# First transfers of a fused transformer-layer kernel cut and reordered, with three matmuls on a cleared region ahead

## What is computed

```python
def rms_norm(x, g):
    y = x * lax.rsqrt(jnp.mean(x * x, axis=-1, keepdims=True) + EPS)
    return y * g

h = rms_norm(x, mix_norm)
z = h @ w_in                      # columns: attn q,k,v | ret q,k,v,gate | gates A,B
aq, ak, av, rq, rk, rv, rg, ga, gr = split(z)
rq, rk = apply_rope(rq), apply_rope(rk)
merged = sigmoid(ga) * attention(aq, ak, av) @ w_o_att + sigmoid(gr) * norm_gate(retention(rq, rk, rv), rg) @ w_o_ret
x = x + merged @ w_out
x = x + peer(rms_norm(x, ffn_norm))                       # top-k experts, gathered
x = x + sigmoid(rms_norm(x, ple_norm) @ w_ple_gate) * (p @ w_ple_proj)
return rms_norm(x, final_norm)
```

## Time and profile before

| | us |
|---|---|
| Median of 3 runs | 1992.97 |
| Lowest and highest | 1991.73 and 1994.1 |
| Profiled execution, whole | 1998.92 |
| Its span (first to last instruction) | 1997.1 |
| TensorE busy in the span | 1961.2 |

### The profile page before, as it was taken

The page is one execution under the profiler, slowest core; times in us unless marked ns, Lnnn a source line. Parts: engine busy times, 40 slices in busy tenths (PEclk is TensorE's granted clock), DMA queues, the critical chain, the costliest instruction groups (busy, mean ns, idle before and its releaser), DMA issues.

```text
span 1997.1 us, 28913 instructions
## 1 busy us (share of the span) xinstructions
PE 1961.2 (98%) x10211; PEld 1725.5 (86%) x10211; DVE 1313.9 (66%) x2287; ACT 803.8 (40%) x1273; POOL 1226.6 (61%) x682
## 2 busy tenths in 40 slices
PE   7999999999999999999999999999999999999997
PEld 6888888888888888999999999999888888888886
DVE  6433333333732389988967888861897898888846
ACT  6222222233553333443345666663343333333352
POOL 5342424243234333898877666667899888888821
PEclk9999999999999999999999999999999999999998
DMA  6232313242223332999987999999999999999921
GB/s 210 74 112 62 115 59 107 72 137 80 80 85 95 103 118 79 332 339 329 353 307 258 392 362 365 372 384 315 350 380 387 370 363 355 366 362 363 357 64 43
DMA packets 171953, 471.93 MB, mean 236 GB/s; under 512 B 13776, under 2 KB 62928, under 8 KB 170064
## 3 DMA queue, kind: packets, MB, share of 16 engines
q1 hardware_dynamic: 58032, 209.04, 30.9%
q0 software_dynamic: 41472, 151.01, 19.9%
q10 hardware_dynamic: 72352, 110.64, 15.8%
HBM read 413.49 MB, written 54.53 MB: 234 GB/s over the span
## 4 chain that ended last, share of the span: by engine, by line
PE 69%; DMA 10%; DVE 9%; POOL 8%; issue 2%; ACT 1%; DVEq 0%; SPq 0%; ACTq 0%; POOLq 0%
PE bank L923 22%; PE bank L925 21%; PE bank L924 21%; DMA xT<-peer_down,scr 9%; POOL w_lo L488 6%; POOL xT L512 3%; DVE xT L1303 3%; PE bank L1031 1%; PE bank L1114 1%; DMA gate_scratch<-scr 1%; PE bank L1099 1%; DVE b_hi L1659 1%; DMA raw<-weights 1%; PE bank L1075 0%; PE bank L1085 0%
## 5 line engine op out<-in xcount | busy, mean ns | idle before, releaser
L488 POOL TENSOR_TENSOR w_lo<-raw,w_hi 128x1024 fp32r<-128x1024 f32 x390 | 936.9, 2411 | 570.1 <-ACT w_hi L538 566.0
L923 PE MATMUL bank<-h_hi,w_hi 128*128 128x352 f32 (+2 forms) x1560 | 550.9, 353 | 9.7 <-ACT scr L743 8.9
L925 PE MATMUL bank<-h_hi,w_lo 128*128 128x352 f32 (+2 forms) x1560 | 539.2, 346 | 0.0
L924 PE MATMUL bank<-h_lo,w_hi 128*128 128x352 f32 (+2 forms) x1560 | 538.2, 345 | 0.0
L538 ACT ACTIVATE w_hi<-raw 128x1024 fp32r<-128x1024 f32 x390 | 405.9, 1053 | 283.1 <-DMA raw<-weights 139.4
L923 PEld LDWEIGHTS bank<-h_hi,w_hi 128*128 128x128 f32 x1560 | 294.4, 189 | 31.9 <-POOL w_lo L488 7.3
L924 PEld LDWEIGHTS bank<-h_lo,w_hi 128*128 128x128 f32 x1560 | 295.3, 189 | 19.8
L925 PEld LDWEIGHTS bank<-h_hi,w_lo 128*128 128x128 f32 x1560 | 293.7, 188 | 20.9
L923 PE MATMUL bank<-w_hi,b_hi 128*128 128x512 f32 x768 | 298.8, 389 | 0.0
L925 PE MATMUL bank<-w_hi,b_lo 128*128 128x512 f32 x768 | 298.8, 389 | 0.0
L924 PE MATMUL bank<-w_lo,b_hi 128*128 128x512 f32 x768 | 298.8, 389 | 0.0
(11 more groups left out here) (215 smaller groups left out, 2446.9 us busy)
## 6 DMA issues: line engine op xcount, KB each, us to landing
raw<-weights SPq DMA_DIRECT2D x390, 512.0 KB, 5.4
act_scratch<-scr ACTq DMA_DIRECT2D x64, 384.0 KB, 5.8
gate_scratch<-scr ACTq DMA_DIRECT2D x12, 2048.0 KB, 12.7
scr<-gate_scratch ACTq DMA_DIRECT2D x22, 768.0 KB, 9.9
scr<-act_scratch ACTq DMA_DIRECT2D x22, 768.0 KB, 15.4
xT<-gate_scratch ACTq DMA_DIRECT2D x10, 768.0 KB, 9.1
xT<-act_scratch ACTq DMA_DIRECT2D x10, 768.0 KB, 13.8
scr<-scr ACTq DMA_DIRECT2D x20, 128.0 KB, 2.9
```

What stands on the lines that cost most here:

```text
L488: return nc.gpsimd.tensor_tensor(w_lo[:, s, :], raw[:, s % RAW, :], w_hi[:, s, :].bitcast(F32), ALU.subtract)
L923: nc.tensor.matmul(out, a_hi, c_hi, start=first, stop=False)
L924: nc.tensor.matmul(out, a_hi, c_lo, start=False, stop=False)
L925: return nc.tensor.matmul(out, a_lo, c_hi, start=False, stop=last)
```

## The change

The first transfers are cut and ordered anew. The norms' factors (columns 384 to 415 of `small`, 16 KB) go first under a semaphore of their own; weight unit 0 follows; x comes in five pieces of 1, 1, 2, 2 and 2 tiles, and weight unit 1 is issued between the third and the fourth; the rest of `small` comes in two pieces behind x, and weight units 2 and 3 last. ACT, DVE and TensorE wait for the parts they need. ACT makes `w_hi` of unit 1 after its sixth tile of x, no longer after the eighth. DVE first writes 1.0 into 640 columns of the scratch region, and TensorE runs three float32 matmuls of 512 columns on them, into a bank that is overwritten later.

```diff
--- before.py
+++ after.py
@@ -127,6 +127,10 @@
 S_AT = [sum(S - P * i for i in range(j)) for j in range(TT)]
 SMALL = 3 * P + 4 * KT + AH + 2 * NKEY
 SCRATCH = 15104
+GAINS = slice(3 * P, 3 * P + 4 * KT)
+X_PARTS = ((0, 1), (1, 2), (2, 4), (4, 6), (6, 8))
+X_PART = [i for i, (a, b) in enumerate(X_PARTS) for _ in range(a, b)]
+WARM = 3
 
 HALVES = (slice(0, S // 2), slice(S // 2, S))
 TD = S - P
@@ -349,8 +353,8 @@
         proj_free, pg_free = [sem("proj_free0"), sem("proj_free1")], sem("pg_free")
         tile_ready, tile_free = sem("tile_ready"), sem("tile_free")
 
-        x_landed = [sem(f"x_landed{i}") for i in range(KT // 2)]
-        small_landed = sem("small_landed")
+        x_landed = [sem(f"x_landed{i}") for i in range(len(X_PARTS))]
+        small_landed, gains_landed, warm_ready = sem("small_landed"), sem("gains_landed"), sem("warm_ready")
         rope_r_landed, rope_a_landed, p_landed = sem("rope_r_landed"), sem("rope_a_landed"), sem("p_landed")
         mask_landed = sem("mask_landed")
         decay_landed = [sem("decay_landed0"), sem("decay_landed1")]
@@ -463,11 +467,15 @@
 
         @block.sync
         def _(sp):
+            sp.dma_start(small[:, GAINS], small_d[:, GAINS]).then_inc(gains_landed, 16)
             sp.dma_start(raw[:, 0, :], w_d[0]).then_inc(landed[0], 16)
-            sp.dma_start(small[:, :], small_d).then_inc(small_landed, 16)
-            for i in range(KT // 2):
-                sp.dma_start(xT[:, 2 * i:2 * i + 2, :], xT_d[:, 2 * i:2 * i + 2, :]).then_inc(x_landed[i], 16)
-            for s in range(1, RAW):
+            for i, (a, b) in enumerate(X_PARTS):
+                sp.dma_start(xT[:, a:b, :], xT_d[:, a:b, :]).then_inc(x_landed[i], 16)
+                if b == 4:
+                    sp.dma_start(raw[:, 1, :], w_d[1]).then_inc(landed[1], 16)
+            for part in (slice(0, GAINS.start), slice(GAINS.stop, SMALL)):
+                sp.dma_start(small[:, part], small_d[:, part]).then_inc(small_landed, 16)
+            for s in range(2, RAW):
                 sp.dma_start(raw[:, s, :], w_d[s]).then_inc(landed[s], 16)
             with sp.Fori(1, NU // RAW) as r:
                 for s in range(RAW):
@@ -592,11 +600,12 @@
                 nc.scalar.activation(h_hi[:, k, :], normed[:, k % 2, :], ACT.Copy).then_inc(h_hi_ready, 1)
 
             run_ahead(0)
-            sc.wait_ge(small_landed, 16)
+            sc.wait_ge(gains_landed, 16)
             for k in range(KT):
-                sc.wait_ge(x_landed[k // 2], 16)
+                sc.wait_ge(x_landed[X_PART[k]], 16)
                 gained_upper(0, k, b_hi)
-            run_ahead(1)
+                if k == 5:
+                    run_ahead(1)
             for k in range(KT):
                 square(0, k)
                 if k == KT // 2:
@@ -604,6 +613,7 @@
             sc.dma_start(rope_r[:, :, :], rope_r_d).then_inc(rope_r_landed, 16)
             for i in range(2):
                 sc.dma_start(decay[:, i, :], decay_d[i]).then_inc(decay_landed[i], 16)
+            sc.wait_ge(small_landed, 32)
             root(0)
             run_ahead(RING - 1)
             for k in range(KT):
@@ -1008,11 +1018,14 @@
                     columns(("wor", i, m), b_hi, b_lo, kt=4, u=UNIT[("wor", 4 * i + m // 2)],
                             at=P * (m % 2), width=2 * P)
 
-            pe.wait_ge(small_landed, 16)
+            pe.wait_ge(warm_ready, 1)
+            for _ in range(WARM):
+                nc.tensor.matmul(bank[:, 7, :], cut(0, P), cut(P, S), start=True, stop=True)
             for i in range(RH):
                 values, gates_r = [("rv", i, t) for t in range(TT)], [("rg", i, t) for t in range(TT)]
                 if i == 0:
                     columns(("rq", 0), b_hi, b_lo, tiles=(u_ready, 0))
+                    pe.wait_ge(small_landed, 32)
                     columns(("rq", 1), b_hi, b_lo, at_tile={KT // 2: lambda: add_up(0), KT - 2: lambda: spread(0)})
                     for key in (("rk", 0), ("rk", 1)):
                         columns(key, b_hi, b_lo)
@@ -1415,10 +1428,12 @@
                 mark(tt(yacc[:, m, :], yacc[:, m, :], z, ALU.mult), tile_free)
 
 
-            ve.wait_ge(small_landed, 16)
+            nc.vector.memset(cut(0, P + S), 1.0).then_inc(warm_ready, 1)
+            ve.wait_ge(gains_landed, 16)
             for k in range(KT):
-                ve.wait_ge(x_landed[k // 2], 16)
+                ve.wait_ge(x_landed[X_PART[k]], 16)
                 gained_lower(0, k, b_lo, b_hi)
+            ve.wait_ge(small_landed, 32)
             for k in range(KT):
                 add_square(0, k)
             norm_scale(0)
```

## The result

| | before | after |
|---|---|---|
| Median of 19 runs each, us | 1991.99 | 1996.70 |
| Lowest and highest | 1987.88 and 1995.4 | 1993.88 and 2006.38 |
| Ratio, 95% interval | | 1.0022 [1.0013, 1.0031] |
| DVE's copy that ends the norm's chain | 24.03 | 27.99 |
| First scores of the retention | 60.08 | 64.00 |

The changed kernel is slower by 0.22% [0.13, 0.31], 4.4 us by the ratio and 4.7 by the medians. The forecast was 1994.8 (+1.85 us) in a range of 1991.0 to 1996.7: the time lies at the range's upper end, and the interval has the bound of 0.2% that was called no change inside it. Measured once more at the end, 7 runs against 17 other runs of the kernel before, it was 1.0026 [1.0014, 1.0038].

What follows compares the result with a forecast made beforehand. The prediction took x landing, ACT's tiles, the norm's chain and DVE's 18 us to bound the beginning, then TensorE to the end. Loads +0.65 and clock +1.2 gave +1.85 on 1992.97, so 1994.8, range 1991.0 to 1996.7.

Steps and rivals of the forecast that it cites:

- The path: At the start: x landing, ACT's tiles, squares, add_up, 1/rms, spread and DVE's 18 us set TensorE's steady work.
- TensorE's earlier start leads nowhere: Early matmuls: an earlier start and full clock gain nothing, as TensorE must follow the tiles; first real matmul 8.2 to 8.8.
- Term 1, the loads: Transfers and ACT's chain: the squares begin later, by +0.4 to +0.9 us, taken as +0.65.
- the landing of the first small pieces: First x transfers: landings follow the bytes ahead at 1.27 us per 512 KB, tiles 2 and 3 at 7.75 to 8.2.
- the overhead that the prediction weighed and left out: Factors' 16 KB transfer: small-transfer overhead, some 2 us, would make the sum 1.6 higher; taken as overlapping.
- Costs nothing by itself: ACT's w_hi of unit 1 between tiles 5 and 6: no cost, ACT's work ahead of the squares being the same sum.
- the waits for `small`: DVE's first sum (14.9) and TensorE's second rq pass (15.5): the waits cost nothing, small landing at 12.8.
- Term 2, the clock: TensorE behind a 2.9 us wait for the sum: half clock slows six matmuls and spread, 0 to +1.7, taken as +1.2.
- The sign given for it: In the profile after: if spread follows add_up by 2.4 us as before, the clock term is wrong.
- The forecast's copy: DVE's copy ending the norm's chain comes at 25.2 to 26.5, where it was at 24.03.
- The rival that forecast 1997.3: TensorE from 18 us on: two slow clock stretches make it last at the normalised tiles; +4.3 us, chance 0.07.
- the head start: ACT's first x tile: begins at 6.0 for 7.32; if it survives, -1.3 us, 1991.7, chance 0.14.

Runs made afterwards that it cites:

- e11: e5 with DVE making the normalised tiles ahead of the second rotation and the first values tile's lower part ahead of the keys' rotation; ratio 0.9992 [0.9978, 1.0006].
- e3: Changed kernel with ACT's w_hi of unit 1 back behind the eighth tile and unit 1's transfer issued behind all of x; ratio 1.0006 [0.9994, 1.0019].
- e5: Changed kernel with unit 1's transfer behind x, its w_hi behind the eighth tile, and the square root's table loaded early; ratio 1.0004 [0.9991, 1.0018].
- e2: Changed kernel with ACT's w_hi of unit 1 back behind the eighth tile, transfer order unaltered; ratio 1.0015 [0.9998, 1.0032].
- e1: Changed kernel with ACT's wait for the rest of small ahead of its three table transfers, not the square root; ratio 1.0020 [1.0008, 1.0031].
- e4: Changed kernel without DVE's fill and the three float32 matmuls; ratio 1.0019 [1.0007, 1.0031].
- e13: Changed kernel once more, unaltered, against other runs of the kernel before; ratio 1.0026 [1.0014, 1.0038].
- e6: Kernel before with DVE making the normalised tiles ahead of the second rotation, and ACT making w_hi of units 6 and 7 between its tiles; ratio 0.9991 [0.9976, 1.0005].
- e10: e6 on the kernel before, with DVE also making the first values tile's lower part ahead of the keys' rotation; ratio 1.0007 [0.9993, 1.0021].
- e12: e10 timed once more, against other runs of the kernel before; ratio 0.9995 [0.9985, 1.0005].
- e8: Kernel before with one more wait of ACT for small ahead of the square root; ratio 1.0005 [0.9993, 1.0018].

## Why the prediction came out as it did

**The path** was right: landing, ACT, squares, sum, 1/rms, `spread`, DVE's 18 us. The shift of the copy (3.96) is the shift at the scores (3.92), and experiments that moved the copy moved the scores by as much. That TensorE's earlier start leads nowhere held too, down to the waits for tiles; its first real matmul is at 8.96, a little past the 8.2 to 8.8 given, as POOL's lower part of unit 0 slows DVE's first two as well (2.55 us for the pair from 6.93).

**Term 1, the loads,** had the right cause and sign and was too small: +1.79 for +0.65 (0.4 to 0.9), or +1.3 by the means of all profiles. The step that failed is the landing of the first small pieces at 1.27 us for each 512 KB. Tiles 2 and 3 landed at 9.2 (7.75 to 8.2 forecast), tiles 4 and 5 at 11.7 (10.3 to 10.7). Between these two, 1024 KB took 2.5 us, so from there on the rate held, and the wait for the latter was right (1.15 for about 1.2); what was lost was lost by 9.2. The 16 KB ahead of everything landed 1.8 us from their issue but moved `w_hi` of unit 0 by 0.07 us only (4.79 for 4.72): the overhead that the prediction weighed and left out overlapped, as it took it to. (The last sum of bytes should read 3412 KB for 3420, which changes nothing.) The transfers of after move less in the first microseconds than those of before; the last number is GB/s, after first, then before:

```profile
4.00:6.00 2.00, 2.00 (x4) 0.67 (x2) 0.00 (x0) 1.06 (x1) 0.07 (x1) 1.00 1.01 281
8.00:10.00 2.00, 1.04 (x3) 0.88 (x4) 1.48 (x2) 0.79 (x2) 0.27 (x1) 0.76 0.99 369
```

```profile
4.00:6.00 2.00, 0.00 (x0) 0.00 (x0) 0.00 (x0) 1.06 (x1) 0.14 (x1) 1.00 0.97 348
8.00:10.00 2.00, 0.92 (x2) 0.83 (x3) 1.82 (x3) 2.00 (x5) 0.20 (x1) 1.00 1.01 414
```

The engines are as busy (1.01 and 0.99) and move a tenth to a fifth less. I had taken the rate of pieces of 512 KB for pieces of 16 and 256 KB. Whether their size or unit 1's transfer beside them is what slows tiles 2 and 3 isn't settled: ACT begins with tile 2 at 8.34 to 8.83 with unit 1 behind x (e11, e3, e5) and at 8.64 to 9.21 with it beside them, all of them later than the forecast.

**"Costs nothing by itself"** was the step that was wrong, of the move of `w_hi` forward. It is true of ACT, the engine that I counted. But the instruction releases POOL, and POOL beside two of DVE's lower parts costs 1.29 us on the path. I had followed the moved instruction on its own engine and queue and not to the engine that waits for it.

**The table** was missing: +0.90. The prediction put the waits for `small` at nothing because it lands at 12.8 ahead of the work they guard, and it named DVE's and TensorE's and not ACT's ahead of the root. `small` is indeed there long before the root. The cost is in what a second wait makes of the first one.

**Term 2, the clock,** +1.2 of 0 to 1.7, was 0 in both profiles of after, and +0.7, +1.5 and +0.7 in e2, e1 and e4. The sign given for it misleads: `spread` follows `add_up` by 3.16 us in after for 2.4 before, at full clock, and it is the table's load. Its mechanism exists and strikes in some executions. The wait was 2.14 us and not 2.9, since the lower parts that POOL held back made `("rq", 0)` late too. The beginning costs 3.96 in this pair (3.6 by the means of the copies: after and e13 against before, e6, e10 and e12) and the whole 4.4 to 4.7; a clock term of 0.7 to 1.5 in part of the runs would account for the difference, but the intervals don't show it.

So the sum of the forecast, 1.85, is 0.65 + 1.2, and that of the run 1.79 + 1.29 + 0.90 + 0. The forecast's copy, 25.2 to 26.5, was missed by 1.5 us. That the time fell into the range was luck, twice over: the range reached to the upper ends of terms that had other sizes, while two of the three real terms were not in it, and it was built on a median of 3 runs, 1992.97, where 19 gave 1991.99. As a difference it reaches to +3.7 us, and measured were +4.4 to +4.7. The rival that forecast 1997.3 had nearly the right number by a mechanism (two slow stretches from 18 us on) that neither profile of after shows. What should have drawn the forecast up was that each part of the change touched the path only to its cost: the prediction itself found no gain in it but the head start, which ACT's wait for tile 2 had already used up.

## What to carry to other kernels

Follow a moved instruction to the engines that it releases, and ask what they will run beside: here 1.3 of 4 us came from a helper that began its work at another moment. A wait added in front of an instruction with hidden preparation (a table load) can move the preparation behind the data, so put it ahead of an earlier instruction. And cut first transfers only if the engine behind them can't catch up by itself: bytes put ahead of the last piece are paid in full, pieces landing sooner aren't.

## What the hardware showed beyond expectation

- Two of DVE's operations with both operands in SBUF take 2.94 us beside POOL's lower part and 1.41 without (one, at 64.59, takes 2.77); the held one ends 0.56 us behind POOL's instruction. Four with one operand in PSUM take 3.10 to 3.11 us either way.
- In the kernel as built, a second wait ahead of an activation that needs a new table puts the first one on the table's load: 0.9 us at the copy, alone (e8).
- One wait of TensorE, of about 2.1 us at one place, is followed by some 3 us at half clock in some executions and not in others (granted clock at 24.2 to 27.4: 1.00, 1.00, 0.50, 0.58 in after, e13, e1, e4). The wait of 2.02 at 500 us was followed by it in before and not in after.
- With pieces of 16 and 256 KB first, the DMA engines moved 271 to 287 GB/s over 2 to 6 us in eight profiles and 299 in e4, with pieces of 340 and 512 KB 307 to 316 in five.
